# Retention's score and state products in three fp32r products, with its q and k kept in the residual's context columns, and an opening in another order

## The reference, cut to what matters

```python
mod_x = (silu_c @ ada_w[i] + ada_b[i])          # 6 x 1024 numbers: shift, scale, gate, twice
hx = modulate(rmsnorm(x, norm1_g[i]), sx1, cx1)
...
q = rope_2d(q, row_pos, col_pos)                # latent q, k; 4 heads of 256
k = rope_2d(k, row_pos, col_pos)
...
scores = jnp.einsum("bhid,bhjd->bhij", qc, kc) * dmask
o = jnp.einsum("bhij,bhjv->bhiv", scores, vc) + jnp.einsum("bhid,bhdv->bhiv", qc, s) * xi
```

## Time and profile before

| | before |
|---|---|
| median of 3 runs | 1705.29 us (1704.89 to 1705.66) |
| profiled execution | 1701.43 us |
| its span, first to last instruction | 1699.6 us |
| TensorE busy | 1656.4 us, 97% |
| VectorE busy | 921.8 us, 54% |
| ScalarE busy | 651.7 us, 38% |
| GpSimd busy | 177.8 us, 10% |
| mean granted TensorE clock | 0.993 |

### The profile page before, as it was taken

How to read it: one execution, slowest core, us unless ns; L and a number is a source line. 1 busy time by engine, 2 the same in 40 slices (tenths; PEclk the granted TensorE clock), 3 DMA queues, 4 the chain that set the end, 5 groups by cost and what they waited for, 6 DMA issues and landing times.

```text
span 1699.6 us, 25132 instructions
## 1 busy us (share of the span) xinstructions
PE 1656.4 (97%) x9862; PEld 1431.4 (84%) x9862; DVE 921.8 (54%) x1471; ACT 651.7 (38%) x980; POOL 177.8 (10%) x191
## 2 busy tenths in 40 slices
PE   6999979999999999999999999999999999999998
PEld 4677748998888888888899888989898888888888
DVE  6799997763424342234368453644445744443444
ACT  4566556542323222222344232312233533332334
POOL 2388872000000000000000000000000000000000
PEclk9999999999999999999999999999999999999999
DMA  9777752222221212222113120211222324333321
GB/s 327 253 248 243 239 185 75 63 75 59 59 81 50 74 54 70 62 62 69 48 46 104 50 78 29 81 50 51 57 64 73 92 73 120 99 98 101 99 87 50
DMA packets 238030, 165.64 MB, mean 97 GB/s; under 512 B 5288, under 2 KB 213016, under 8 KB 237944
## 3 DMA queue, kind: packets, MB, share of 16 engines
q1 hardware_dynamic: 234088, 150.43, 29.3%
q0 software_dynamic: 2992, 10.88, 2.0%
q10 hardware_dynamic: 864, 3.15, 0.5%
HBM read 162.34 MB, written 2.10 MB: 97 GB/s over the span
## 4 chain that ended last, share of the span: by engine, by line
PE 82%; DVE 13%; DMA 2%; ACT 1%; issue 1%; POOL 0%; DVEq 0%; ACTq 0%
PE ps L648 82%; DVE ps L1787 3%; DVE ps L1804 3%; DVE w_lo L1585 2%; DMA ada_more<-in_ada_w 1%; DVE H_lo L1626 1%; DVE rstd L1591 1%; DMA ada<-in_ada_w 0%; DVE tmp L1614 0%; DVE ps L1802 0%; ACT tmp L1323 0%; DVE sq L1614 0%; DVE conv L1886 0%; DVE ps L1784 0%; DMA conv<-in_x 0%
## 5 line engine op out<-in xcount | busy, mean ns | idle before, releaser
L648 PE MATMUL ps<-H_hi,w_hi 128*128 128x512 f32 (+1 forms) x1712 | 586.5, 343 | 14.3 <-DVE H_lo L1688 6.9
L648 PE MATMUL ps<-H_lo,w_hi 128*128 128x512 f32 (+1 forms) x1712 | 580.5, 339 | 0.0
L648 PE MATMUL ps<-H_hi,w_lo 128*128 128x512 f32 (+1 forms) x1712 | 580.0, 339 | 0.0
L648 PEld LDWEIGHTS ps<-H_hi,w_hi 128*128 128x128 f32 x1712 | 326.3, 191 | 70.0 <-issue 29.4
L1585 DVE TENSOR_TENSOR w_lo<-w_raw,w_hi 128x1024 fp32r<-128x1024 f32 x208 | 255.2, 1241 | 192.5 <-ACT w_hi L1146 159.6
L648 PEld LDWEIGHTS ps<-H_hi,w_lo 128*128 128x128 f32 x1712 | 326.4, 191 | 35.1
L648 PEld LDWEIGHTS ps<-H_lo,w_hi 128*128 128x128 f32 x1712 | 326.8, 191 | 34.4
L648 PE MATMUL ps<-mid_hi,w_hi 128*128 128x512 f32 (+1 forms) x592 | 199.4, 337 | 0.6
L648 PE MATMUL ps<-mid_lo,w_hi 128*128 128x512 f32 (+1 forms) x592 | 198.3, 335 | 0.0
L648 PE MATMUL ps<-mid_hi,w_lo 128*128 128x512 f32 (+1 forms) x592 | 198.0, 335 | 0.0
L2057 DVE SCALAR_TENSOR_TENSOR tmp<-ps,par,tmp 128x511 f32<-128x511 f32 x66 | 41.6, 658 | 231.3 <-ACT tmp L1484 155.0
(11 more groups left out here) (239 smaller groups left out, 1931.6 us busy)
## 6 DMA issues: line engine op xcount, KB each, us to landing
w_raw<-in_ffn_w_in SPq DMA_DIRECT2D x88, 512.0 KB, 3.8
ada<-in_ada_w SPq DMA_DIRECT2D x40, 1024.0 KB, 6.2
w_raw<-in_ret_w_in SPq DMA_DIRECT2D x40, 512.0 KB, 3.9
w_raw<-in_ffn_w_out SPq DMA_DIRECT2D x32, 512.0 KB, 4.4
w_raw<-in_conv_pw_w SPq DMA_DIRECT2D x22, 512.0 KB, 8.6
w_raw<-in_ffn_w_out SPq DMA_DIRECT2D x16, 384.0 KB, 3.5
ada<-in_ada_w POOLq DMA_DIRECT2D x4, 1024.0 KB, 14.1
w_raw<-in_ret_w_out SPq DMA_DIRECT2D x8, 512.0 KB, 4.1
```

Source lines behind the costliest of these rows:

```text
L648: return nc.tensor.matmul(o, a, b, start=first, stop=last, skip_group_check=True)
```

## The change

In the retention:
- The rotated q and k, the decayed q of direction two and `y_tok` move from `qT` and `kT` into the context columns of the residual `X` (`q32`, `k32`), 4 pieces of 256 columns each, 768 apart. `qT`, `kT` and `state` are gone.
- The scores are made in three fp32r products. The parts of q are in the last head's rows of `y_hi` and `y_lo`, those of k in new `kq_hi` and `kq_lo`. ScalarE writes the high parts (`qk_hi_ready`), VectorE the low ones (`qk_lo_ready`), for which TensorE waits.
- So are the products with the state. Its parts are put in the place of those of q once all four scores are done (`score_done` + 5 instead of + 3); the parts of the decayed q of direction one are put in the place of those of k, and those of direction two in that same place when direction one's products are done. TensorE waits for `qd_lo_ready`.

In the opening, TensorE:
- `ada_products(2)` stands behind one k tile of the gate half instead of two, `ada_products(3)` ahead of the value half's first k tile instead of behind it, `ada_products(4)` ahead of the gate half's last two k tiles instead of behind them.

VectorE: the first tile's shift stands ahead of the first weight split, and its low part directly behind it; `split_lo(2)` stands behind all of H instead of between the sums of groups 2 and 3. ScalarE: `split_hi(2)` and `split_hi(3)` stand behind the fifth and seventh tile of H, `ada_copy(4)` behind the eighth without a wait for the low parts, and writes another buffer.

The diff, without the lines that make the five new semaphores:

```diff
--- before.py
+++ after.py
@@ -198,11 +198,10 @@
             y_lo = sb("y_lo", [P, KT, LAT], F32R, ph)
-            qT = sb("qT", [P, 2, LAT], F32, ph)
-            kT = sb("kT", [P, 2, LAT], F32, ph)
+            kq_hi = sb("kq_hi", [P, 2, LAT], F32R, ph)
+            kq_lo = sb("kq_lo", [P, 2, LAT], F32R, ph)
             V = sb("V", [P, LT, DH], F32, ph)
             scores = sb("scores", [P, 2, 10 * P], F32, ph)
-            state = sb("state", [P, 2, 2, DH], F32, ph)
             decay = sb("decay", [P, 2, LAT], F32, ph)
@@ -210,7 +209,16 @@
-        y_tok = qT[:].rearrange("p f t -> p (f t)").rearrange("p (t v) -> p t v", t=LT)
+        y_tok = k32 = X[:, 0:LT, LAT:TOK]
+        q32 = X[:, LT:2 * LT, LAT:TOK]
+        last_y = slice(2 * HEADS - 2, 2 * HEADS)
+
+        def in_tiles(buf):
+
+            return buf.rearrange("p f (a n) -> p (f a) n", n=CTX)
+
+        qs_hi, qs_lo = in_tiles(y_hi[:, last_y, :]), in_tiles(y_lo[:, last_y, :])
+        ks_hi, ks_lo = in_tiles(kq_hi[:]), in_tiles(kq_lo[:])
         flat_tmp, flat_sq = (a[:].rearrange("p a b -> p (a b)") for a in (tmp, sq))
@@ -233,7 +241,7 @@
                 return rstd[:, 0:GROUP * P]
-            beside = not isinstance(m, int) or m <= 20
+            beside = not isinstance(m, int) or 4 < m <= 20
             return flat_tmp[:, 2 * TOK - GROUP * P:] if beside else ada_row0[:]
@@ -897,18 +910,19 @@
                 pe.wait_ge(slot_read[p], S_PW1 // 2)
-            first_block(0, 0, 2)
+            first_block(0, 0, 1)
             ada_products(2)
-            first_block(0, 2, 4)
+            first_block(0, 1, 3)
             ada_transposes(2)
+            first_block(0, 3, 4)
             pe.wait_ge(par_ready, 2)
+            ada_products(3)
             first_block(1, 0, 1)
-            ada_products(3)
-            first_block(1, 1, 2)
             ada_transposes(3)
-            first_block(1, 2, 4)
-            first_block(0, KT // 2, KT)
+            first_block(1, 1, 4)
+            first_block(0, KT // 2, KT - 2)
             ada_products(4)
+            first_block(0, KT - 2, KT)
             first_block(1, KT // 2, KT)
@@ -1092,7 +1106,7 @@
-                pe.wait_ge(rot_step, 15 * h + 15)
+                pe.wait_ge(qk_lo_ready, 2 * h + 2)
                 for j in range(LT):
@@ -1101,7 +1115,11 @@
                     for f in range(2):
-                        m = mm(ps[:, 6 + j % 2, :], kT[:, f, j * P:(j + 1) * P], qT[:, f, :], f == 0, f == 1)
+                        q_hi, q_lo = y_hi[:, 2 * HEADS - 2 + f, :], y_lo[:, 2 * HEADS - 2 + f, :]
+                        k_hi, k_lo = kq_hi[:, f, j * P:(j + 1) * P], kq_lo[:, f, j * P:(j + 1) * P]
+                        mm(ps[:, 6 + j % 2, :], k_hi, q_hi, f == 0, False)
+                        mm(ps[:, 6 + j % 2, :], k_hi, q_lo, False, False)
+                        m = mm(ps[:, 6 + j % 2, :], k_lo, q_hi, False, f == 1)
                     m.then_inc(score_done, 1)
@@ -1113,7 +1131,7 @@
                     pe.wait_ge(score_read, (h + 1) * LT)
-                    pe.wait_ge(qdec_ready, 2 * h + d + 1)
+                    pe.wait_ge(qd_lo_ready, 2 * h + d + 1)
                     for i in range(LT):
@@ -1122,7 +1140,11 @@
                         for f in range(2):
-                            m = mm(o, (q_dec if d == 0 else kT)[:, f, i * P:(i + 1) * P], state[:, d, f, :], False, f == 1)
+                            qd_hi, qd_lo = kq_hi[:, f, i * P:(i + 1) * P], kq_lo[:, f, i * P:(i + 1) * P]
+                            s_hi, s_lo = (a[:, 2 * HEADS - 2 + d, f * DH:(f + 1) * DH] for a in (y_hi, y_lo))
+                            mm(o, qd_hi, s_hi, False, False)
+                            mm(o, qd_hi, s_lo, False, False)
+                            m = mm(o, qd_lo, s_hi, False, f == 1)
                     m.then_inc(score_done, 1)
@@ -1238,10 +1260,11 @@
             ada_copy(3)
-            split_hi(2, 2)
             for j in range(KT // 2, KT):
                 first_hi(j)
-
+                if j in (4, 6):
+                    split_hi(j // 2, j // 2)
+            ada_copy(4)
             act.wait_ge(h0_lo_ready, KT)
@@ -1274,8 +1297,6 @@
-            split_hi(3, 3)
-            ada_copy(4)
             gates(0)
@@ -1535,22 +1556,26 @@
                     decays()
+                act.wait_ge(rot_step, 15 * h + 7)
+                A(qs_hi, q32, ACT.Copy).then_inc(qk_hi_ready, 1)
                 split_hi(u + 6, (u + 6) % RING)
+                act.wait_ge(rot_step, 15 * h + 15)
+                A(ks_hi, k32, ACT.Copy).then_inc(qk_hi_ready, 1)
...
                 A(V[:].rearrange("p a b -> p (a b)"), ps[:, 0:2, :].rearrange("p a b -> p (a b)"), ACT.Copy)
-                act.wait_ge(rot_step, 15 * h + 15)
                 A(vctx.rearrange("p a b -> p (a b)"), ps[:, 2, :], ACT.Copy).then_inc(slot_read[0], 1)
...
-                act.wait_ge(score_done, 7 * h + 3)
-                A(state[:].rearrange("p d f v -> p (d f v)"), ps[:, 3:5, :].rearrange("p a b -> p (a b)"),
-                  ACT.Copy).then_inc(slot_read[1], 1)
+                act.wait_ge(score_done, 7 * h + 5)
+                A(y_hi[:, last_y, :], ps[:, 3:5, :], ACT.Copy).then_inc(state_hi_ready, 1)
...
                 A(decay[:, 1, :], iota[:], ACT.Exp, scale=ngam[:, ab[1]], bias=lgam512[:, ab[1]]).then_inc(decay_exp, 1)
+                act.wait_ge(qdec_ready, 2 * h + 1)
+                A(kq_hi[:], q_dec, ACT.Copy).then_inc(qd_hi_ready, 1)
                 for d in range(2):
@@ -1566,6 +1591,10 @@
                     A(gn_mv[:, :, 1], gn_mv[:, :, 1], ACT.Sqrt, bias=eps[:, 1:2]).then_inc(gn_std, 1)
+                    if d == 0:
+                        act.wait_ge(score_done, 7 * h + 6)
+                        act.wait_ge(qdec_ready, 2 * h + 2)
+                        A(ks_hi, q32, ACT.Copy).then_inc(qd_hi_ready, 1)
             y_parts(HEADS - 1)
@@ -1742,15 +1771,17 @@
             first_modulation(2, 0)
+            first_shifted(0)
             split_lo(0, 0)
-            first_tiles(range(KT // 2))
+            first_lo(0)
+            first_tiles(range(1, KT // 2))
             split_lo(1, 1)
...
             ada_sum(2, 0, FIRST_GROUPS[2])
-            split_lo(2, 2)
             ada_sum(3, 0, FIRST_GROUPS[3])
...
             first_tiles(range(KT // 2, KT))
+            split_lo(2, 2)
             split_lo(3, 3)
@@ -2117,7 +2148,8 @@
                             dve.wait_ge(rot_step, n_at + 2 + a)
-                    v.tensor_tensor(dst[:, f, :], cosd, rot, ALU.add).then_inc(rot_step, 1)
+                    halves = (a.rearrange("p (a n) -> p a n", n=CTX) for a in (cosd, rot))
+                    v.tensor_tensor(dst[:, 2 * f:2 * f + 2, :], *halves, ALU.add).then_inc(rot_step, 1)
@@ -2146,12 +2178,14 @@
                     dve.wait_ge(yT_done, h)
-                rotate(0, qT, DH ** -0.5, 15 * h, s // 2 + 1)
+                rotate(0, q32, DH ** -0.5, 15 * h, s // 2 + 1)
                 split_lo(u + 5, (u + 5) % RING)
...
                     ages_of()
+                dve.wait_ge(qk_hi_ready, 2 * h + 1)
+                v.tensor_tensor(qs_lo, q32, qs_hi.bitcast(F32), ALU.subtract).then_inc(qk_lo_ready, 1)
                 split_lo(u + 6, (u + 6) % RING)
@@ -2162,12 +2196,14 @@
                     dve.wait_ge(zeta_ready, 2 * HEADS)
-                rotate(1, kT, 1.0, 15 * h + 7)
+                rotate(1, k32, 1.0, 15 * h + 7)
                 for t in range(CT):
...
                 o.then_inc(slot_read[1], 1)
+                dve.wait_ge(qk_hi_ready, 2 * h + 2)
+                v.tensor_tensor(ks_lo, k32, ks_hi.bitcast(F32), ALU.subtract).then_inc(qk_lo_ready, 1)
                 split_lo(u + 7, (u + 7) % RING)
@@ -2184,15 +2220,24 @@
                 dve.wait_ge(rot_step, 15 * h + 15)
-                for d, dst in enumerate((q_dec, kT[:])):
-                    v.tensor_tensor(dst, qT[:], decay[:, d, :].unsqueeze(1).to_broadcast([P, 2, LAT]), ALU.mult) \
-                        .then_inc(qdec_ready, 1)
+                for d, dst in enumerate((in_tiles(q_dec), q32)):
+                    by_token = decay[:, d, :].rearrange("p (a n) -> p a n", n=CTX).unsqueeze(1) \
+                        .to_broadcast([P, 2, LAT // CTX, CTX])
+                    split = (a.rearrange("p (f a) n -> p f a n", f=2) for a in (dst, q32))
+                    v.tensor_tensor(*split, by_token, ALU.mult).then_inc(qdec_ready, 1)
+                dve.wait_ge(state_hi_ready, h + 1)
+                v.tensor_tensor(y_lo[:, last_y, :], ps[:, 3:5, :], y_hi[:, last_y, :].bitcast(F32), ALU.subtract) \
+                    .then_inc(slot_read[1], 1)
+                dve.wait_ge(qd_hi_ready, 2 * h + 1)
+                v.tensor_tensor(kq_lo[:], q_dec, kq_hi[:].bitcast(F32), ALU.subtract).then_inc(qd_lo_ready, 1)
                 for d in range(2):
...
                     else:
+                        dve.wait_ge(qd_hi_ready, 2 * h + 2)
```

(1 more changed line is left out.)

## The result

The changed kernel takes 1688.97 us (median of 6 executions, 1685.73 to 1690.59), the kernel before 1703.47 in the same comparison (1701.37 to 1705.66). The ratio is 0.9913, 95% interval 0.9902 to 0.9924, and the difference of the medians 14.5 us, where 16.0 were forecast, and a median of 1689.3. The profiled execution of the changed kernel took 1689.13 us with a span of 1687.3.

What follows compares the result with a forecast made beforehand. TensorE's matmuls were taken to bound retention, VectorE's chain of taps the opening and convolution. Retention's 10.3 us plus the opening's 5.7 made 16.0 us off 1705.29, so 1689.3 us, range 1685.5 to 1695.5.

Steps and rivals of the forecast that it cites:

- Pace and scores: Retention scores: 64 f32 records at 0.430 us become 96 fp32r records at 0.2272 us, 5.7 us off.
- State products: Retention state products: 128 f32 records at 0.2156 us become 192 fp32r at 0.120, 4.6 us off; changes of kind free.
- Parts in time: Retention: high and low parts ready before TensorE; 4 us left at state, 4.5 direction two, 0.3 third score.
- The rival of waits: Retention: parts come later than TensorE for the state or third score; 8 us lost, 1697 us; chance 0.08.
- points 1 to 3: Opening: transposes at 43.1 us, modulation's second half at 44.1, TensorE waits 1.2 for tile 5, last H_lo at 52.1.
- Point 2: Opening: a weight split no longer ahead of the reduction, another 1.35 us; modulation's second half at 44.1, first H_lo 46.7.
- the open point: Opening: whether the new 1.2 us stop lowers TensorE's clock; taken as no fall; chance of opening giving less 0.19.
- points 4 and 5: Opening: first block done at 54.1, taps 4.4 us sooner, a 1.26 us VectorE wait gone; 5.7 us gained.
- Point 5: Opening: sixth group's DMA lands at 59.3, TensorE comes at 58.8; VectorE's 1.26 us wait at the second block goes.
- Sum: Whole kernel: 10.3 + 5.7 = 16.0 us off, giving 1685.4 us profiled and 1689.3 us median.
- the same mechanism at half its price, no change: Retention: fp32r and f32 products alternating on TensorE cost half the slower case's price per change; no change; chance 0.02.

Runs made afterwards that it cites:

- lengthening: Changed kernel with six more subtractions per head ahead of the low part of the decayed q: 1707.18 us, ratio 1.0011 to the kernel before.
- the filled kernels: 16 unread fp32r products put in the 2.20 us stop before the last feed-forward part: 1686.08 us on the changed kernel, 1703.54 us on the kernel before.

## Why the prediction was right, step by step

- **Pace and scores.** 0.229 us a record, and 5.6 us by the kernel with f32 scores, against 5.7. Shown.
- **State products.** 0.12 us a record, 4.7 us against 4.6. Nothing for a change of kind. Shown by the spacing and by what the f32 scores leave.
- **Parts in time.** Slack 4.2 and 4.6 us where 4.0 and 4.5 were forecast, and 4.2 again by lengthening; no idle time of TensorE at scores, third scores or state products in the profile. The rival of waits is out.
- **Opening, points 1 to 3.** First stop 4.11 (3.8 forecast), the fourth group's transposes at 43.40 (43.1), new stop 0.97 (1.2), last H_lo done at 52.5 (52.1). Point 2 was mis-sized: it took 1.35 us for the split of weights. From the transposes to the reduction were 46.83 - 45.13 = 1.70 us before and are 44.04 - 43.40 = 0.64 now, as the reduction then waits for the transposes: 1.06. So the modulation, forecast for 44.1, is there at 44.67, and the first H_lo at 47.3 instead of 46.7:

```profile
44.67 1.31 ACT L1255 ACTIVATE H_hi<-conv,mod,gain 128x512 fp32r<-128x512 f32 x2 [1.69 <-DVE gain L1699]
```

  The clock behind the new stop was the open point. It stayed full in all eleven profiled executions with the new order (a stop of 0.97 us in eight, of 0.62 in three) and fell in all three with the old one and its 2.3 us stop (the window from 50 to 60 us: 0.84, 0.66 and 0.66). Of the kernel before and the changed one:

```profile
50.00:60.00 10.00, 9.88 (x47) 5.99 (x48) 5.77 (x16) 4.90 (x7) 0.00 (x0) 0.84 0.57 143
```

```profile
50.00:60.00 10.00, 10.00 (x67) 7.24 (x70) 6.33 (x15) 4.42 (x8) 0.00 (x0) 1.00 0.88 273
```

- **Opening, points 4 and 5.** Here lies the rest of the miss: from the last H_lo to the end of the first block were 2.6 us, not 2.0, so that the block was done at 55.1, not 54.1, as ScalarE's row says, which waits for it:

```profile
55.15 1.28 ACT L1297 ACT_TABLE_LOAD   x1 [1.71 <-PE ps L661]
```

  The table load has only moved behind that wait and still stands ahead of the sigmoid; but VectorE's first write is released by TensorE's value block, not by the gate. So taps began 0.9 us later than forecast, and the profiles give 5.0 us instead of 5.7. Point 5 came true: the sixth group's products begin at 59.61 without a stop. The kernel before was at the lucky end there: its opening's context write was at 86.8, 88.1 and 89.2 in three executions, the new one's at 81.4 to 82.6 in the seven that have it unaltered. Their means are 6.2 us apart. Both stops of the opening have a part in it. Behind the first one the clock was half in all eleven profiles that leave it unfilled, until between 34.5 and 38 us, and the reduction moves with it: 43.57 to 44.64 us in the new order, 46.83, 46.92 and 47.68 in the old. The rest comes behind the 2.3 us stop. This is read from the profiles; no kernel filled that stop alone.
- **Sum.** 16.0 forecast, 14.5 by the medians, 15.6 by the fastest of the filled kernels and 17.5 by their medians. The mechanisms were right, and what was off is a term that the sum lacked: the clock behind the 2.20 us stop at the start of the last feed-forward part, 0 to 2.7 us, drawn anew in each execution in both kernels. The median is then one of a mixture, and its agreement within 0.3 us is luck: the sum was 1.5 us too large, and the 1705.29 from which it was taken lay 1.8 us above the 1703.47 of the larger sample. For the profiled execution the same sum said 1685.4, and it took 1689.13: the two traces are 12.3 us apart, not 16.0, of which 0.7 belong to the opening, 0.4 to the stretch at 270 us and 2.6 to the clock at the last part. The prediction took 3.9 us between a profiled execution and the median as a plain offset. The trace had the stop of 2.20 us, which can make up to 2.7 of it, and the clock in the opening, where the context write of the other two executions came 1.3 and 2.4 us later.
- **A slip that changed nothing.** The chance for "the same mechanism at half its price, no change" doesn't fit the sum: the whole gain is gone at 0.25 us for a change of kind, and half of 0.3 us would leave 6.4.

## What to carry to other kernels

Where a product's kind is changed under an engine that is never idle, distances between starts give its worth to a tenth of a microsecond, and the slack of what feeds it can be read as a difference of two rows and tested by lengthening. Before a profiled execution is compared with a median, look for stops of TensorE of a microsecond or more: behind each the clock may or may not fall, and a difference of 2 or 3 us between two executions can be that alone. Such a stop is worth filling with products that nobody reads if they end before what is waited for; price them by the record first, since an f32 product is two.

## What the runs showed of the hardware

- One and the same stop of 2.20 us, with the same rows around it, was followed by full clock twice and by half clock seven times in unfilled profiled executions; filled down to 0.28 or 0.29 us it was followed by full clock in all four profiles. The half clock cost 1.2 to 2.7 us.
- The first stop of the opening, 3.8 to 4.6 us, was followed by half clock in all eleven profiles that leave it unfilled, and by full clock in the three with products in it.
- A later stop of 0.97 us in the opening left the clock full in eight profiles, one of 1.23 us at the start of the last part was followed by half clock in its one profile. Whether length or place decides stays open.
- Four stops of 3.34 us, otherwise alike, were followed by half clock three times: where the heads' distances give it, such a wait cost 3.6 us with the clock full behind it, 5.0 and 6.2 with the clock fallen.
- A row of f32 products and fp32r products in turn runs as fast as each alone, to 0.01 us at a change.
